# A two-layer transformer block on one core: half of the shared expert's work moved into the expert loop

## The reference

```
s      = sigmoid(x @ router_w)                      # 256 x 64
gate   = top 6 of 64 experts per token, normalised, x 2.5
routed = sum over chosen experts e of gate * ((silu(x @ w_gate[e]) * (x @ w_up[e])) @ w_down[e])
shared = (silu(x @ sh_gate) * (x @ sh_up)) @ sh_down
x      = layer_norm(ALPHA * x + routed + shared)
```

## Time and profile before

| | |
|---|---|
| three runs | 1364.78, 1369.56, 1377.91 us; median 1369.56 us |
| the profiled execution | 1365.9 us, of it 1364.1 us span |
| PE busy | 1240.6 us (91%), mean granted clock 0.958 of full speed |
| DVE, ACT busy | 366.7 us (27%), 254.8 us (19%) |
| transfers | 444.16 MB; of it 3 x 128 expert weights of 1024 KB |
| chain that ended last | PE 83%; gate/up L644 33%, down L664 17% |

### The profile page before, as it was taken

One profiled execution on the slowest core, in us unless ns is written; L12 is line 12 of the kernel. 1 busy time (PEld: TensorE's weight loads), 2 busy tenths in 40 slices (PEclk: granted clock), 3 DMA queues, 4 the chain that ended last, 5 costly groups with the idle time before them and its releaser, 6 DMA issues.

```text
span 1364.1 us, 16120 instructions
## 1 busy us (share of the span) xinstructions
PE 1240.6 (91%) x6183; PEld 581.0 (43%) x6183; DVE 366.7 (27%) x751; ACT 254.8 (19%) x532; POOL 16.0 (1%) x22
## 2 busy tenths in 40 slices
PE   7988989999999999999968888999999999999994
PEld 3565454334343443434334654434434343443431
DVE  0376452112121221212132245312212121221214
ACT  0025221111111111111112532111111111111110
POOL 0000000000000000000000001000000000000000
PEclk9978989999999999999979888999999999999997
DMA  9551052999999999999963604199999999999992
GB/s 335 189 208 70 1 224 116 411 422 421 421 422 422 422 421 422 422 422 422 425 244 120 247 1 192 35 414 420 422 421 422 422 422 422 421 422 422 422 421 93
DMA packets 67556, 444.16 MB, mean 326 GB/s; under 512 B 7617, under 2 KB 11969, under 8 KB 16193
## 3 DMA queue, kind: packets, MB, share of 16 engines
q1 hardware_dynamic: 67520, 443.66, 79.3%
HBM read 442.59 MB, written 1.05 MB: 325 GB/s over the span
## 4 chain that ended last, share of the span: by engine, by line
PE 83%; DVE 7%; ACT 5%; issue 4%; DMA 1%; POOL 1%; POOLq 0%; SPq 0%; DVEq 0%
PE psum L644 33%; PE psum L664 17%; PE psum L614 5%; PE psum L739 4%; PE psum L534 4%; PE psum L688 4%; PE psum L563 2%; PE psum L674 2%; DVE arena L1355 2%; PE psum L832 1%; ACT arena L968 1%; ACT room L954 1%; PE psum L479 1%; PE psum L858 1%; PE psum L627 1%
## 5 line engine op out<-in xcount | busy, mean ns | idle before, releaser
L644 PE MATMUL psum<-ring,room 128*64 128x512 f32 x2048 | 457.3, 598 | 23.2 <-issue 23.2
L644 PEld LDWEIGHTS psum<-ring,room 128*64 128x64 f32 x2048 | 168.4, 138 | 302.5 <-issue 302.5
L664 PE MATMUL psum<-ring,arena 128*64 128x512 f32 x1024 | 233.9, 597 | 4.7 <-issue 2.4
L1364 DVE TENSOR_TENSOR y_low<-psum,y_high 128x1024 fp32r<-128x1024 f32 x64 | 78.4, 1224 | 359.9 <-ACT y_high L961 359.9
L664 PEld LDWEIGHTS psum<-ring,arena 128*64 128x64 f32 x1024 | 75.9, 136 | 132.0 <-issue 122.6
L1355 DVE SCALAR_TENSOR_TENSOR arena<-arena,psum 128x256 f32<-128x256 f32 x64 | 30.7, 480 | 357.9 <-ACT arena L968 357.9
L961 ACT CAST y_high<-psum 128x1024 fp32r<-128x1024 f32 x64 | 64.8, 1012 | 254.5 <-PE psum L664 254.5
L968 ACT ACTIVATE arena<-psum 128x256 f32<-128x256 f32 x64 | 24.6, 384 | 418.6 <-PE psum L644 418.6
L614 PE MATMUL psum<-onehot,x_high 128*128 128x256 f32 x256 | 78.2, 331 | 5.9 <-ACT room L954 3.1
L688 PE MATMUL psum<-y_high,spread 32*128 32x512 f32 x512 | 65.2, 499 | 5.0 <-issue 4.9
L614 PE MATMUL psum<-onehot,x_low 128*128 128x256 f32 x256 | 67.6, 288 | 0.0
(11 more groups left out here) (214 smaller groups left out, 879.7 us busy)
## 6 DMA issues: line engine op xcount, KB each, us to landing
ring<-in_expert_w_gate SPq DMA_DIRECT2D x128, 1024.0 KB, 14.4
ring<-in_expert_w_up SPq DMA_DIRECT2D x128, 1024.0 KB, 16.5
ring<-in_expert_w_down SPq DMA_DIRECT2D x128, 1024.0 KB, 15.5
ring<-in_swa_nsa_w_in SPq DMA_DIRECT2D x8, 1036.0 KB, 16.1
room<-in_swa_nsa_w_out SPq DMA_DIRECT2D x1, 4096.0 KB, 18.1
room<-in_mla_w_out SPq DMA_DIRECT2D x1, 4096.0 KB, 16.1
ring<-in_mla_w_in SPq DMA_DIRECT2D x1, 2688.0 KB, 13.2
ring<-in_mla_w_uq SPq DMA_DIRECT2D x1, 2304.0 KB, 8.2
```

What stands on the lines that cost most here:

```text
L644: mm = pe.matmul(BANK[2][CAP * e:CAP * e + CAP, :], xg[:, c, 2 * j + e, :], expert(slot[j % NPAIR * 2 + e])[0][:, c], start=c == 0, stop=c ...
L664: mm = pe.matmul(PS[0][CAP * e:CAP * e + CAP, half * 512:(half + 1) * 512], ht[:, c, CAP * e:CAP * e + CAP], expert(slot[j % NPAIR * 2 + e ...
L1364: V.tensor_tensor(ylo, PS[0][:, :], yhi.bitcast(F32), ALU.subtract).then_inc(sem[f"yd_dve{L}"], 1)
```

## The change

- `pe_shared` is split. Gate/up for the first 128 tokens stays ahead of the loop (`pe_shared_up(pe, L, 0)`), and directly behind it come the rank matmuls. Gate/up for the other 128 tokens and both transpositions go into step 12 (the first of group 3), ahead of that step's gate/up; the combination of step 11 is moved ahead of it as well.
- Both down products go to the head of step 20 (the first of group 5).
- DVE takes the ranks and the one-hot tile first; the shared product and the number of groups come after that.
- Gate/up of step 0 waits chunk by chunk for the gathered rows, not for all eight.
- Groups 3, 4 and 5 are written out; loops stand over groups 1 and 2 and over group 6. The number of groups is read after group 0.
- SP: the shared down weight is loaded behind expert 3, the mixture's constants ahead of it; the parameters of the second layer norm are loaded behind the last refill, into the space of the shared gate weight.
- Buffers are placed anew; rows are gathered into `arena`, the y tiles lie in `lnp`.

```diff
+SHARED_UP, SHARED_DOWN = 3, 5
...
-            load_shared(sp, L)
+            load_gate_up(sp, wbig, s_gate[L], s_up[L], sem["shared_in"])
+            sp.dma_start(mcon, moe_const).then_inc(sem["moec_in"], 16)
             load_expert(sp, L, 3, 3)
-
-            sp.dma_start(mcon, moe_const).then_inc(sem["moec_in"], 16)
-            sp.wait_ge(sem["lnmix_dve"], TC * (L + 1))
-            norm_loads(sp, "ln_ffn_in", ln_ffn_g, ln_ffn_b, L)
+            sp.dma_start(shared_down, s_down[L].rearrange("(p c) n -> p (c n)", c=DE // P)).then_inc(sem["shdown_in"], 16)
             sp.wait_ge(sem["groups_dve"], L + 1)
             refills(sp, L)
+            sp.wait_ge(sem["sgu_pe"], TC * (L + 1))
+            norm_loads(sp, "ffn", ln_ffn_g, ln_ffn_b, L)
...
-        def groups(eng, group):
-
+        def groups(eng, L, group):
+
+            group(0, False)
+            eng.wait_ge(sem["groups_dve"], L + 1)
             n_groups = pass_groups(eng)
-            group(0, False)
-            with eng.Fori(1, n_groups - 1) as i:
+            with eng.Fori(1, SHARED_UP) as i:
+                group(i, False)
+            for i in range(SHARED_UP, SHARED_DOWN + 1):
+                group(i, False)
+            with eng.Fori(SHARED_DOWN + 1, n_groups - 1) as i:
                 group(i, False)
             group(n_groups - 1, True)
...
             pe_gather(pe, L, 0)
-            pe_shared_down(pe, L, 0)
             pe_slots(pe, L, 0)
...
+                    if shared_step(i, j, SHARED_UP):
+                        pe.wait_ge(sem[f"h_dve{L}"], p)
+                        pe_shared_up(pe, L, 1)
+                        pe_combine(pe, L, p - 1, before, 0)
+                        pe.wait_ge(sem[f"ht_act{L}"], p)
+                        pe_shared_turn(pe, L, 0)
+                        pe_combine(pe, L, p - 1, before, 1)
+                        pe_shared_turn(pe, L, 1)
+                        pe_gate_up(pe, L, i, j)
+                        pe_turn(pe, L, p, i + 1)
+                        pe_down(pe, L, i, j, last)
+                        continue
+                    if shared_step(i, j, SHARED_DOWN):
+                        for tc in range(TC):
+                            pe_shared_down(pe, L, tc)
...
         def pe_moe_steps(pe, L):
-            pe_shared(pe, L)
+            pe_shared_up(pe, L, 0)
+            pe_rank(pe, L)
             pe_experts(pe, L)
...
                 dve.wait_ge(sem["rank_pe"], L + 1)
-                link(V.tensor_reduce(most, BANK[2][:, TC * NE:2 * TC * NE], AX_X, ALU.max))
-                link(V.tensor_tensor(over, most.to_broadcast([P, 3]), mcon[:, M_PASS:M_PASS + 3], ALU.is_gt))
-                link(V.tensor_reduce(most, over, AX_X, ALU.add))
-                mark(V.tensor_scalar(more_groups[:, :], most, float(GROUPS), None, ALU.mult), "groups_dve")
...
                 settle("rank_dve")
                 pick(0)
+                shared_gated(0)
+                link(V.tensor_reduce(most, BANK[3][:, TC * NE:2 * TC * NE], AX_X, ALU.max))
+                link(V.tensor_tensor(over, most.to_broadcast([P, 3]), mcon[:, M_PASS:M_PASS + 3], ALU.is_gt))
+                link(V.tensor_reduce(most, over, AX_X, ALU.add))
+                mark(V.tensor_scalar(more_groups[:, :], most, float(GROUPS), None, ALU.mult), "groups_dve")
```

More of the change, by code:

```diff
@@ L553, in pe_logits, with pe_shared_up, pe_rank @@
             mm.then_inc(sem["logit_pe"], 1)
-        def pe_shared(pe, L):
+        def pe_shared_up(pe, L, tc):
             gu = v(wbig[:, 0:2 * KC * DE], m=2, c=KC, f=DE)
[L559 to L565, removed]
+            pe.wait_ge(sem["shared_in"], BOTH["shared_in"] * (L + 1))
+            for c in range(KC):
+                mm = pe.matmul(v(BANK[2], m=2, f=DE), xcol[:, c, tc * P:(tc + 1) * P], gu[:, :, c, :],
+                               start=c == 0, stop=c == KC - 1)
+            mm.then_inc(sem["sgu_pe"], 1)
+        def pe_rank(pe, L):
             pe.wait_ge(sem["gate_dve"], L + 1)
@@ L597, in groups, with shared_step @@
             return n_groups
+        def shared_step(i, j, step):
+            return isinstance(i, int) and i == step and j == 0
         def pe_gather(pe, L, i, p=None):
@@ L671, in pe_turn @@
             pe.wait_ge(sem[f"gates_dve{L}"], gates)
+            if isinstance(p, int) and p == SHARED_UP * GP:
+                pe.wait_ge(sem["sht_act"], TC * (L + 1))
             pe.wait_ge(sem[f"h_dve{L}"], p + 1)
@@ L688, in pe_combine @@
                     mm = pe.matmul(ACC[tc][:, half * 512:(half + 1) * 512], spread[rows, j, tc * P:(tc + 1) * P],
-                                   part[rows, half * 512:(half + 1) * 512], start=False, stop=last and turn == 1 and part is ylo)
+                                   part[rows, half * 512:(half + 1) * 512],
+                                   start=isinstance(p, int) and p == 0 and turn == 0 and part is yhi, stop=last and turn == 1 and part is ylo)
                     if last and turn and part is ylo and q >= 2:
@@ L710, in group @@
                         pe_gather(pe, L, i + 1, p)
[L711 to L714, removed]
+                    if not first:
+                        pe_combine(pe, L, p - 1, before, 0)
                     pe_turn(pe, L, p, i + 2 if ahead else i + 1)
                     if not first:
-                        pe_combine(pe, L, p - 1, (j - 1) % 2, 1)
+                        pe_combine(pe, L, p - 1, before, 1)
                     pe_down(pe, L, i, j, last)
-            n_groups = groups(pe, group)
+            n_groups = groups(pe, L, group)
             for turn in range(2):
@@ L944, in act_moe, with shared_silu, shared_turned @@
         def act_moe(act, L):
-            for tc in range(TC):
+            def shared_silu(tc):
                 act.wait_ge(sem["sgu_pe"], TC * L + tc + 1)
-                nc.scalar.activation(ssg[tc], BANK[tc][:, 0:DE], ACT.Silu).then_inc(sem["ssilu_act"], 1)
+                nc.scalar.activation(ssg[tc], BANK[2][:, 0:DE], ACT.Silu).then_inc(sem["ssilu_act"], 1)
+            def shared_turned():
+                act.wait_ge(sem["sht_pe"], TC * (L + 1))
+                for tc in range(TC):
+                    nc.scalar.copy(sht[tc], v(BANK[3][:, tc * 256:tc * 256 + 256], c=2, t=P)).then_inc(sem["sht_act"], 1)
             def x_gathered(i):
@@ L975, in turned @@
                 nc.scalar.copy(ht, v(BANK[3][:, 0:2 * P], c=2, t=P)).then_inc(sem[f"ht_act{L}"], 1)
-            for tc in range(TC):
-                act.wait_ge(sem["sht_pe"], TC * L + tc + 1)
-                nc.scalar.copy(sht[tc], v(BANK[3 - tc][:, 0:2 * P], c=2, t=P)).then_inc(sem["sht_act"], 1)
+            shared_silu(0)
             x_gathered(0)
@@ L989, in group @@
                     y_high(p)
-            groups(act, group)
+            groups(act, L, group)
         @block.scalar
@@ L1148, in layer_norm @@
             def layer_norm(L, part):
+                lng, lnb = norm[part]
                 dve.wait_ge(sem[f"ln_{part}_in"], 32 * (L + 1))
@@ L1384, in group @@
                         y_low(p)
-                groups(dve, group)
+                groups(dve, L, group)
             dve.wait_ge(sem["x_in"], 32)
```

94 lines of the change are left out of this document (52 added, 42 removed).

## The result

The changed kernel took 1363.06 us (median of 18 runs, 1359.5 to 1370.0) beside 1373.87 us for the kernel before on the same occasions: ratio **0.9934, interval 0.9919 to 0.9949**, 9.1 us faster. The way was right, the size was not. The profiled execution took 1367.8 us (span 1366.0), longer than that of before, which had been a quick one: by the start of the mixture (the matmuls of line 438, before 441) it was already 5.7 us behind, in the attention of layer 0, whose instructions the change leaves alone (granted clock 0.68 in 100 to 150 us there, 0.81 before). So stages are compared here from that mark on, not spans.

The account below looks back on a forecast made before the run. The prediction took the stream of weights at 422 GB/s to set the pace. Its terms, -21.6 - 1.4 + 9.6 = -13.4 us against the profiled 1365.9, gave 1352.5, or 1356.2 by the median; it said 1355, range 1344 to 1367.

Parts of the forecast that it names:

- Parts 1 to 3: Start of the mixture: gather 7.7 us earlier, first copy 0.5 late, shared down product's 3.4 gone; 21.6 us over both layers.
- Part 4: Step 0 shrinks from 15.0 to about 12.5 us and the stream's thin spot goes: 0.7 us gained per layer.
- Part 5: Step 12 lets its slots go 8.8 us later, the queue forgives 6.2: 2.6 us lost per layer.
- rival C: Loop: PE becomes the bound; 1371 us in full, about 1363 with half of its spare time lost; chance 0.19.
- Part 6: Step 20 grows by 7.06 us, with 1.4 left over, against 6.2 forgiven: 2.3 us lost, last step's tail unchanged.
- Part 7: SP's queue, reordered loads and reading the number of groups: all hidden, costing nothing.
- rival D: Written-out groups: instruction fetches stall PE, 1405 us; gain and loss equal at 4.4 us of stall per group; chance 0.07.
- Rivals B: Loop: the moved work is free because the stream does not run dry, 1343 to 1347 us; chance 0.14.

Follow-up runs that it names:

- the repeat: The changed kernel, unaltered, run and profiled once more on another occasion, against the kernel before: ratio 0.9935, 1363.29 us.

## Why the prediction was wrong

- **What bounds the kernel**: right. The stream of weights sets the pace; every experiment's loop is 454 to 456 us plus what its stream lost (less the 0.7 that the kernel before loses as well).
- **Parts 1 to 3, the start**: 21.6 us said, 23.4 measured. The gather began 7.8 us earlier (7.7 said) in layer 0 and took 6.2 us. Short by 1.8 because the shared product no longer waits for ACT's exponential (0.45 us per layer), which I had overlooked, and because the gather ran at full clock in layer 0 (granted clock 1.00 over it, 0.75 before).
- **Part 4, step 0**: 0.7 us per layer; the data of step 11 are there 155.4 us after step 0's start, before 156.2. Right.
- **Part 5, step 12: this is the term that failed.** 2.6 us said; 6.1 and 6.2 in the first profile, 4.3 and 5.9 in the second. The mechanism was the one forecast, down to the landing in 4.8 us; the size was not, and in three places. PE's extra was 9.3 us, not 8.8, since each of the two pairs of transpositions takes 0.43. Step 11, behind its wait of 1.98 us, ran for part of its time at the lower clock in three of four layers, 1.7 us more; I had that row as the last step's and put it with rival C instead of ahead of step 12. And a queue that runs empty gives less than the arithmetic of landings says: with 9.3 + 1.7 + 0.1 late and 6.2 forgiven 4.9 should lack, 6.1 did. It forgave 5 us in every hole of the table. The difference shows at the ragged edges (221 and 98 going, 147 and 328 coming back); what makes them was not tested.
- **Part 6, step 20**: 2.3 said, 2.0 and 2.2 measured, and that is luck. I had 1.4 us left over from step 12 and 6.2 forgiven. PE waited for data again at step 19 (0.42 and 0.92 us), so nothing was left over: step 20 released 7.2 us late and the queue forgave 5.1 to 5.3. The two errors cancel. "The tail is unchanged" holds for layer 0; in layer 1 the last step ran at the lower clock for a part, and from its start to the end it was 1.5 us longer in the first profile and 1.2 in the second.
- **Part 7, "all nothing"**: right for SP's queue, wrong for the written-out groups. They cost 0.3% in the kernel before, which I had as rival D only from 4.4 us of stall per group on. The Trainium skill, "Runtime: NRT & Kernel Launch", section "Instruction fetch mechanics", has straight code prefetched while the page before runs; here the fetches are in the trace (15 for 6), and the kernel with straight code was slower.
- **Sum**: 23.4 + 1.4 - 2 x 8.2 (mean of four layers, holes of both kinds) = 8.4 us, less some 1.3 for the longer tail of layer 1, 7; measured 9.1 with 2 either way. The 3 us of written-out code have no room in this sum; why they show in the kernel before and hardly here stays open. Rivals B and C are excluded: in layer 0 PE waited for data in steps 7, 10, 11, 19, 27, 30 and 31, and the holes were there.

## What to carry to other kernels

Where a stream of transfers sets the pace, work of the engine that frees the buffers is free only as far as the queue ahead of the next issue is deep: read from issue-to-landing times, step by step, take off what an empty queue needs (here this said 6.2 us and 5 were forgiven), and compare with the whole delay that the engine has collected by then, a slow clock included. Put such work behind the instruction that frees the larger buffer, not ahead of it: 0.9861 for 0.9934 with the same work, of which up to 1.7 us per layer is the clock of the last step. Ask also which step comes next with less to forgive, and whether the last step, whose time nothing hides, will start behind a longer wait.

## What the hardware showed that I had not expected

After a wait of the same length, 1.97 to 2.00 us, the same gate/up product took 7.09 us in some layers and 8.78 in others. The granted clock of the stretch tells why: 0.81 of full speed on average over the slow one, so that it ran for a part at 1.2 in place of 2.4 GHz. Changed kernel, step 11: first profile, layer 0, then the repeat, layer 0.

```profile
369.90:378.70 8.80, 8.80 (x33) 3.23 (x33) 0.33 (x1) 0.00 (x0) 0.00 (x0) 0.81 1.02 424
```

```profile
371.40:378.50 7.10, 7.09 (x33) 2.70 (x33) 0.34 (x1) 0.00 (x0) 0.00 (x0) 1.00 1.01 421
```

Over all profiles, step 11 was slow in 12 of 25 layers behind waits of 1.94 to 2.00 us. The last step was slow in 14 of 18 layers behind waits of 1.95 to 1.99 us and in none of 10 behind waits of 0.3 to 1.1 us. What decides between the two behind the longer wait stays open; a forecast should hold both.
